# Moving the split activations and the split weights of a two-block transformer kernel to other SBUF offsets modulo 512 bytes

## The reference, cut to what matters

```
def swiglu(h, w13, w2):
    gu = jnp.einsum('bsd,df->bsf', h, w13)
    g, u = jnp.split(gu, 2, axis=-1)
    return jnp.einsum('bsf,fd->bsd', jax.nn.silu(g) * u, w2)
...
x = x + 0.5 * mod[:, 0, 2][:, None, :] * swiglu(h, ffn_w13[l, 0], ffn_w2[l, 0])
...
y = hybrid_mixer(h, cos, sin, w_in[l], ...)
...
kv = (hn_ctx @ w_in[i][:, KV_START:]).reshape(b, n_ctx, 2, N_NA_HEADS, NA_HEAD_DIM)
...
h_lat = h_lat + g2 * (jnp.square(jax.nn.relu(hn @ mlp_w1[i])) @ mlp_w2[i])
```

## The kernel before

| tile | before | after |
|---|---|---|
| X, H_HI, H_LO | 128 | 128 |
| A_HI, A_LO | 192 | 128 |
| RAW | 192 | 128 |
| W_HI, W_LO | 192 | 384 |
| C_HI, C_LO, CTOK | 256 | 128 |
| IDENT, ONES | 0 | 192 |
| SQ, UN, RINV | 192 | 256 |
| SSUM, the scratch region (GBUF, GATES, attention tiles) | 256 | 256 |

## Time and profile before

### The profile page before, as it was taken

One profiled execution on the slowest core, in us unless ns is written; L12 is line 12 of the kernel. 1 busy time (PEld: TensorE's weight loads), 2 busy tenths in 40 slices (PEclk: granted clock), 3 DMA queues, 4 the chain that ended last, 5 costly groups with the idle time before them and its releaser, 6 DMA issues.

```text
span 1830.3 us, 23671 instructions
## 1 busy us (share of the span) xinstructions
PE 1794.8 (98%) x8305; PEld 1437.9 (79%) x8305; DVE 1121.0 (61%) x1952; ACT 650.5 (36%) x939; POOL 79.8 (4%) x64
## 2 busy tenths in 40 slices
PE   5999999999999999999999999999999999999998
PEld 2888888887778778787888888988678888888887
DVE  6777668555745655459968953579575363434343
ACT  3442222233246552344222343433354342313232
POOL 2000000010000000200000000200000200000002
PEclk9999999999999999999999999999999999999999
DMA  8766466333323202537656532363300223333331
GB/s 274 221 208 215 154 201 199 109 102 112 82 69 92 69 1 67 164 100 222 188 180 184 173 92 88 111 185 93 58 1 12 81 87 98 92 103 91 93 92 46
DMA packets 361486, 219.98 MB, mean 120 GB/s; under 512 B 11576, under 2 KB 358724, under 8 KB 361412
## 3 DMA queue, kind: packets, MB, share of 16 engines
q1 hardware_dynamic: 361412, 219.03, 40.3%
HBM read 216.91 MB, written 2.11 MB: 120 GB/s over the span
## 4 chain that ended last, share of the span: by engine, by line
PE 94%; DVE 3%; DMA 1%; SPq 1%; issue 1%; ACT 1%; DVEq 0%; ACTq 0%
PE bank L645 26%; PE bank L647 26%; PE bank L646 26%; PE bank L772 3%; PE bank L675 2%; PE bank L676 2%; PE bank L679 2%; PE bank L762 1%; PE bank L830 1%; PE bank L977 1%; DVE GACC L1407 1%; PE bank L697 1%; PE bank L978 1%; PE bank L927 1%; PE bank L807 1%
## 5 line engine op out<-in xcount | busy, mean ns | idle before, releaser
L645 PE MATMUL bank<-H_HI,W_HI 128*128 128x512 f32 x1304 | 515.2, 395 | 1.0 <-DVE W_LO L1383 1.0
L647 PE MATMUL bank<-H_HI,W_LO 128*128 128x512 f32 x1304 | 514.3, 394 | 0.0
L646 PE MATMUL bank<-H_LO,W_HI 128*128 128x512 f32 x1304 | 514.3, 394 | 0.0
L1075 ACT ACTIVATE W_HI<-RAW 128x1024 fp32r<-128x1024 f32 x279 | 293.5, 1055 | 492.8 <-PE bank L647 467.2
L1383 DVE TENSOR_TENSOR W_LO<-RAW,W_HI 128x1024 fp32r<-128x1024 f32 x282 | 345.8, 1227 | 90.0 <-ACT W_HI L1075 80.7
L645 PEld LDWEIGHTS bank<-H_HI,W_HI 128*128 128x128 f32 x1304 | 243.6, 187 | 62.1 <-issue 2.0
L647 PEld LDWEIGHTS bank<-H_HI,W_LO 128*128 128x128 f32 x1304 | 243.6, 187 | 61.0
L646 PEld LDWEIGHTS bank<-H_LO,W_HI 128*128 128x128 f32 x1304 | 243.6, 187 | 60.4 <-issue 0.2
L645 PE MATMUL bank<-A_HI,W_HI 128*128 128x512 f32 x736 | 287.1, 390 | 0.0
L646 PE MATMUL bank<-A_LO,W_HI 128*128 128x512 f32 x736 | 286.4, 389 | 0.0
L647 PE MATMUL bank<-A_HI,W_LO 128*128 128x512 f32 x736 | 286.4, 389 | 0.0
(11 more groups left out here) (266 smaller groups left out, 1684.6 us busy)
## 6 DMA issues: line engine op xcount, KB each, us to landing
RAW<-in_ffn_w SPq DMA_DIRECT2D x120, 512.0 KB, 4.8
GBUF<-in_w_ada SPq DMA_DIRECT2D x33, 1024.0 KB, 6.9
RAW<-in_mlp_w SPq DMA_DIRECT2D x64, 512.0 KB, 3.8
RAW<-in_w_in SPq DMA_DIRECT2D x57, 512.0 KB, 3.9
GBUF<-in_ada_w SPq DMA_DIRECT2D x24, 1024.0 KB, 6.9
RAW<-in_w_out SPq DMA_DIRECT2D x16, 512.0 KB, 3.6
RAW<-in_ffn_w SPq DMA_DIRECT2D x16, 384.0 KB, 3.1
RAW<-in_w_branch SPq DMA_DIRECT2D x8, 512.0 KB, 3.6
```

The source lines that it names most:

```text
L645: pe.matmul(dst, w_hi, x_hi, start=first and i == 0, stop=False)
L646: pe.matmul(dst, w_hi, x_lo, start=False, stop=False)
L647: mm = pe.matmul(dst, w_lo, x_hi, start=False, stop=last and i == len(blocks) - 1)
L1075: act.activation(strip_of(W_HI, slot), strip_of(RAW, slot), ACT.Copy).then_inc(hi_ready, 1)
```

## The change

Small tiles change their places in the order of the `sb` calls, so that A's tiles and RAW come to H's offset modulo 512 bytes and the two weight tiles to an offset 256 bytes from it. The context's tiles are shifted inside the scratch region (by 384 bytes) to H's offset. Two asserts fix these relations, and one assert on the tile RPB, which reaches 64 bytes past `H_LO`, is loosened. No instruction is added, removed or moved; every tile keeps its size.

```
         place[0] += 64
+        COL3 = sb("COL3", [P, 2 * CK2])
+        CSIL = sb("CSIL", [P, 3 * KC])
+        RMS = sb("RMS", [P, 2 * TT])
         A_HI = sb("A_HI", [P, KC * S], F32R)
         A_LO = sb("A_LO", [P, KC * S], F32R)
         RAW = sb("RAW", [P, RING * STRIP])
+        SUM32 = sb("SUM32", [P, 32])
+        CRAW = sb("CRAW", [P, 3 * KC])
         W_HI = sb("W_HI", [P, RING * STRIP], F32R)
         W_LO = sb("W_LO", [P, RING * STRIP], F32R)
...
         scratch = place[0]
+        assert (where["A_HI"] - where["H_HI"]) % 512 == 0 and (where["W_HI"] - where["H_HI"]) % 512 == 256
+        shift = (where["H_HI"] - scratch) % 512
...
-        CTOK = sb("CTOK", [P, 2 * D], over=scratch + 51 * 1024)
-        C_HI = sb("C_HI", [P, KC * CTX], F32R, over=scratch + 35 * 1024)
-        C_LO = sb("C_LO", [P, KC * CTX], F32R, over=scratch + 43 * 1024)
+        CTOK = sb("CTOK", [P, 2 * D], over=scratch + 51 * 1024 + shift)
+        C_HI = sb("C_HI", [P, KC * CTX], F32R, over=scratch + 35 * 1024 + shift)
+        C_LO = sb("C_LO", [P, KC * CTX], F32R, over=scratch + 43 * 1024 + shift)
...
-        assert where["RPB"] + H * SPAN_IN * 4 + 64 == where["A_HI"]
+        assert where["RPB"] + H * SPAN_IN * 4 + 64 <= where["COL3"]
```

More of the change, by code:

```diff
@@ L135, in block_pair_kernel @@
         COL1 = sb("COL1", [P, V_ROWS + 1])
-        CRAW = sb("CRAW", [P, 3 * KC])
         COL2 = sb("COL2", [P, M_CTX])
-        COL3 = sb("COL3", [P, 2 * CK2])
-        CSIL = sb("CSIL", [P, 3 * KC])
         IDENT = sb("IDENT", [P, P])
@@ L142, in block_pair_kernel @@
         FLIP = sb("FLIP", [P, P])
-        SUM32 = sb("SUM32", [P, 32])
         MOD = sb("MOD", [P, M_COLS])
@@ L154, in block_pair_kernel @@
         DIAG = sb("DIAG", [P, S], over=where["RINV"])
-        RMS = sb("RMS", [P, 2 * TT])
         SG = sb("SG", [P, 2 * S], over=where["SQ"])
```

## The result

| | before | after |
|---|---|---|
| median | 1831.4 us (1830.23 to 1832.2, 4 runs) | 1805.38 us (1804.36 to 1806.23, 4 runs) |
| ratio after to before | | 0.9857, 95% interval 0.9843 to 0.9871 |
| span of the profiled execution | 1830.3 us | 1802.1 us |

The changed kernel is faster by 1.4%, 26 us. The forecast was 1820 us in a range of 1796 to 1848: right in sign and in range, wrong in size, since 11 us were forecast. Of the rivals, "the distance decides, and 0 and 256 are alike" (1803 us) is the one that came.

A forecast was written before the change was run, and what follows sets the result against it. TensorE's matmul pace, busy 98% of the span, was taken as the bound. H -17.1, A +5.7 and C 0 sum to -11.4 us on 1830.3, making 1818.9; the median lies 1.0 above: 1820 us, range 1796 to 1848.

The forecast's parts named there:

- the distance decides, and 0 and 256 are alike: Rival for H and A streams: H comes to A's pace, A stays, -28.5 us, 1803 us; chance 0.17.
- What bounds the kernel: TensorE, busy 98% of the span: matmul pace goes one to one into time; H, A and C make 1519.9 us.
- C's term: C's 192 matmuls: cost above half of 215 is 10 ns, at most about 2 us either way; taken as 0.
- The case at 1725 us: Rival for the matmul streams, that a distance of 256 ends the cost: down to 1725 us; chance 0.14.
- The plain float32 matmuls: Plain float32 matmuls on TensorE: the change was costed at nothing for them.
- What depends on the place alone?: Last matmuls without a load, H 397 ns, A 388: most of the difference is the moving tile's own.
- The term for H: H's matmuls: from 233.3 to 229.3 ns, taken from one load at a far distance; 4272 x -4.0 = -17.1 us.
- The 32-column strip: Test of distance dependence on a strip whose weight blocks begin at 64, 192, 320, 448 in turn, each load 109 ns.
- The term for A: A's matmuls: same place and distance as H afterwards, 229.3 in place of 226.7 ns; 2208 x +2.6 = +5.7 us.
- Nothing happens: Rival for H and A: both paces belong to something else, such as high address bits; 1831 us, chance 0.10.

The follow-up runs named there:

- the four kernels with split distances: Changed kernel with W_LO alone off; high and low parts apart; only H_LO off; W_LO moved so streams suit their loads: 1831.0, 1843.6, 1818.0, 1846.3 us.
- the first half alone: Against the kernel before, A, RAW and weights come to H's offset, nothing between RAW and W_HI, C at distance 0: 1804.89 us, ratio 0.9855.

## Why the prediction was right or wrong

**What bounds the kernel** was right: the pace of H, A and C, times their counts, gives the whole difference of the spans.

**Two terms of the sum were taken from no run.** C's term takes 215 ns for the pace of 512 columns without any cost of place, and half of it for 256. No run shows such a pace: in all kernels no H or A stream goes below 226.7 ns, and C's matmuls took 117.8 ns before and 119.9 after. The case at 1725 us has the same 215 in it. The plain float32 matmuls were costed at nothing by the earlier trace rows, a single distance (both operands lie at 192); that term came out right. The same stream in the changed kernel, where the two tiles (TSIN and UC) lie 128 bytes apart modulo 512:

```profile
1297.64 1.02 PE L929 MATMUL bank<-TSIN,UC 128*128 128x512 f32 x2
...
1301.07 1.02 PE L929 MATMUL bank<-TSIN,UC 128*128 128x512 f32 x2
```

That is 3.43 us over 8 records where the earlier trace rows have 3.44, and the mean distance between starts in these streams is 429.1 ns in both kernels and in all twelve of the experiments, with UC 0, 64, 128, 192, 256 and 320 bytes on from TSIN.

**The step that failed is "What depends on the place alone?"** It read the last matmul of a stream, with no load beside it, as a measurement of the place: H 397 ns, A 388, so "most of the difference is the moving tile's own, and A is moved to the place of the slower tile". In the changed kernel H has kept its place; a last H matmul of it, which starts at 816.82 us (window 817.05 to 817.10), with the loads before and after it:

```profile
L649 PE MATMUL bank<-H_HI,W_LO 128*128 128x512 f32 x1 | 0.4, 388 | 0.0
...
816.59 0.19 PEld L649 LDWEIGHTS bank<-H_HI,W_LO 128*128 128x128 f32 x1
818.45 0.19 PEld L647 LDWEIGHTS bank<-H_HI,W_HI 128*128 128x128 f32 x1 [1.67 <-issue]
```

Again no load beside it, and 388 ns instead of 397. The same holds for all last H matmuls with no load in the 0.3 us after their start: five of five take 397 in the kernel before, seven of seven 388 in the changed one. And in the kernel with A at a distance of 64, a last A matmul (starts at 736.37, window 736.60 to 736.65, next load at 737.01) takes what H took:

```profile
L650 PE MATMUL bank<-A_HI,W_LO 128*128 128x512 f32 x1 | 0.4, 397 | 0.0
...
737.01 0.19 PEld L678 LDWEIGHTS bank<-H_HI,W_HI 128*128 128x128 f32 x1 [0.69 <-DVE W_LO L1386]
```

So the place does not set the duration without a load: at H's unchanged place it fell with the distance. It is no clean measure of the distance either. In the same kernel another last A matmul, at 1055.24 us, takes 390, and last H matmuls at a distance of 448 take 388 or 397. The absence of the next load took away one of the possible partners, and I concluded that none was left; the matmul's own load and whatever the stream before it left behind were still there, and which of them acts is not shown. The A matmul with a 64-off load beside it, which kept A's pace, could not decide between place and distance: its own weights lay at 0.

**The term for H was mis-sized**: -4.0 ns forecast, -6.67 measured (17.1 against 28.5 us). It rested on one matmul beside one load of ONES, at a distance of 384, which I called the easiest way to be wrong. A stream that really runs at a distance of 384 has 232.4 ns, not the 229.3 that this record promised; a single record next to a change of load gives neither sign nor size for a stream. In the kernel before, a load 128 or 384 on from H came with a shorter H record, 390 against 394; in the changed kernel a load of SSUM 128 on from A comes with a longer A record, 396 against the 388 of one with no load beside it (starts at 727.19).

**The 32-column strip**, 5.33 us over 23, 231.7 ns, was read as showing that the distance hardly matters. Its blocks step through 64, 192, 320 and 448, which are 64 and 192 of a period of 256, so it never came to the one narrow place where the pace is better (226.7 ns at 0 and 256), and the test could not see it. But it would have shown little there either: in the changed kernel the blocks step through 256, 384, 0 and 128, half of them at the good distance, and the strip (matmuls that start at 434.01 and 439.32) goes at 5.31 us over 23, 231 ns, where the mean of 226.7 and 232.4 is 229.6. A strip whose distance changes from block to block does not stand for a stream at one distance.

**The term for A** (+5.7 us) fell with the place: it is 0. It and the 11.4 us by which the term for H was short are the missing 17 us. **C** was costed at 0 and took +0.4 us, inside its bound.

**The rivals.** "0 and 256 are alike" was right in its forecast (1803), and 226.7 ns at both distances bears it out; but steps of 128 are not what the pace goes by: 128 and 384 have 232.4, and the four pairs show a period of 256. "256 ends it" (down to 1725) is refuted by the 226.7 ns at 256 and the 1805.38 us. "Nothing happens" is refuted: the same matmuls go at 226.7 or 233.3 ns by nothing but the distance between the two operands that TensorE reads.

**What stays open.** That the distance modulo 256 sets the pace when all parts have one distance, and the place does not, is shown. How it does so is not: the matmul's own operands, the pair of stream and load beside it, and the same pair booked one record later each failed on at least one of the four kernels with split distances. Yet the place of the next load comes in too. In the changed kernel a matmul beside which SSUM is loaded has its own weights at 256 and SSUM 128 on from its moving tile; one of them:

```profile
1433.76 0.40 PE L649 MATMUL bank<-A_HI,W_LO 128*128 128x512 f32 x1
1433.99 0.51 PE L705 MATMUL bank<-ONES,SSUM 128*128 128x1 f32 x4
```

All four such records of the changed kernel, three of A and one of H, take 396 ns, and the next start comes 233 to 234 ns later. In the kernel with all places 64 bytes on, where SSUM lies 64 on from A and H, the four take 388 and the next start comes after 226 to 227. SSUM's distance from the weights loaded before it changes along with that from the moving tile (both 128, then both 64, modulo 256), so the two cannot be told apart. Whether the distance from one load to the next, or from one moving tile to the next, comes in was not tried by itself. Nor is it shown why 256-column streams want another distance than 512-column ones.

## What to carry to other kernels

When one inner loop bounds a kernel, compare its pace between tiles that run the same code; a steady difference of some 3% (here 233.3 against 226.7 ns), indifferent to all other engines (173 matmuls in 40 us with VectorE busy for 27.8 or for 17.6), may be an effect of addresses and then can be won by moving tiles, here by putting moving and stationary tiles at one offset modulo 256 bytes (H at 226.7 ns, 1831.4 us to 1805.38). Measure such an effect by steady streams, and move one distance at a time: a single odd record in the trace, even one that repeats five times (397 ns), is no measurement of a stream. Padding put in for another reason (here 64 bytes for an overhang, which left H 64 bytes off) can be the cause, and half of an edit may be all that works (1804.89 us with the first half alone).

## What the runs showed of the hardware

- With the moving and the stationary tile at one offset modulo 256 bytes, a stream of 512-column float32r matmuls, each with its own 128 by 128 load, went at 226.7 ns; 32 bytes off on either side (224 and 288) at 233.3; at 192, 228.9. With 256 columns, 119.9 ns at 0 and 116.7 to 118.6 at the other distances tried, in the first of three streams.
- Moving both tiles together by 64 bytes changed nothing (226.7 ns, 1805.2 us, against 226.7 and 1805.38).
- Splitting the distances between the high and low parts can cost more than either distance alone: 234.5 ns with A_HI at 320 and A_LO at 256, against 233.3 with all at 320 and 226.7 with all at 256; 232.0 with H_HI at 256 and H_LO at 192, against 226.7 and 228.9.
- A matmul whose own weights lie at 256 took 396 ns where the next load (SSUM) lay 128 bytes on from the moving tile and from those weights, modulo 256, and 388 ns where it lay 64 on (four records in each kernel).
